# Splitting the expert matrices into high and low parts, slab by slab, in a routed expert layer

## The reference, cut to what matters

```python
s = jax.nn.sigmoid((t @ router_w).astype(jnp.float32))
...
combine = jnp.sum(jax.nn.one_hot(idx, N_EXPERTS, dtype=jnp.float32) * w_sel[..., None], axis=1).astype(dt)
y = jnp.zeros_like(t)
for e in range(N_EXPERTS):
    h = jax.nn.silu(t @ w_gate[e]) * (t @ w_up[e])
    y = y + combine[:, e:e + 1] * (h @ w_down[e])
```

## Time and profile before

| | us |
|---|---|
| median of 3 runs | 3338.19 (3337.83 to 3340.89) |
| the profiled execution | 3339.61 |
| its span | 3337.7 |
| PE busy | 2944.3 (88%) |
| DVE busy | 1571.7 (47%) |
| ACT busy | 962.6 (29%) |
| Pool busy | 383.8 (12%) |
| mean granted TensorE clock | 0.939 of full |

### The profile page before, as it was taken

How to read it: one execution, slowest core, us unless ns; L and a number is a source line. 1 busy time by engine, 2 the same in 40 slices (tenths; PEclk the granted TensorE clock), 3 DMA queues, 4 the chain that set the end, 5 groups by cost and what they waited for, 6 DMA issues and landing times. The chain is left out here.

```text
span 3337.7 us, 56931 instructions
## 1 busy us (share of the span) xinstructions
PE 2944.3 (88%) x25160; PEld 2565.6 (77%) x25160; DVE 1571.7 (47%) x2624; ACT 962.6 (29%) x1623; POOL 383.8 (12%) x238
## 2 busy tenths in 40 slices
PE   6999899898998989998998989989796567699994
PEld 5998898898998979988888989989585554344442
DVE  4633345437886246333454368862378644100003
ACT  4321335323332143213243233321332133001102
POOL 2210121220110002101211101110000100000000
PEclk8999999999998989999999999989897878799997
DMA  6210221462333222102214423332131000888862
GB/s 258 75 43 28 75 76 56 148 220 98 135 133 98 94 80 77 41 28 77 74 56 137 131 89 133 133 110 89 60 95 38 0 19 0 340 341 308 328 224 83
DMA packets 92842, 386.47 MB, mean 116 GB/s; under 512 B 10288, under 2 KB 11312, under 8 KB 85296
## 3 DMA queue, kind: packets, MB, share of 16 engines
q1 hardware_dynamic: 68112, 313.09, 27.0%
q10 hardware_dynamic: 16704, 41.36, 3.4%
q0 software_dynamic: 7776, 28.32, 2.3%
HBM read 332.46 MB, written 50.27 MB: 115 GB/s over the span
## 5 line engine op out<-in xcount | busy, mean ns | idle before, releaser
L307 PE MATMUL PS<-HR,HIGHR 128*128 128x264 f32 x3008 | 864.9, 288 | 0.0
L307 PE MATMUL PS<-XR,HIGHR 128*128 128x264 f32 (+1 forms) x1792 | 570.1, 318 | 48.0 <-DVE HR L1386 14.2
L307 PEld LDWEIGHTS PS<-HR,HIGHR 128*128 128x128 f32 x3008 | 577.9, 192 | 2.9
L307 PE MATMUL PS<-XR,RINGR 128*128 128x264 f32 x1600 | 463.6, 290 | 0.0
L307 PE MATMUL PS<-ARENA 64*64 64x64 f32 (+8 forms) x8640 | 399.6, 236 | 72.1 <-DVE ARENA L2000 43.5
L307 PE MATMUL PS<-HH,HIGHR 128*128 128x264 f32 x1536 | 441.2, 287 | 24.2 <-DVE HR L1603 24.2
L291 ACT CAST HIGHR<-RING 128x1024 fp32r<-128x1024 f32 (+2 forms) x340 | 330.8, 977 | 396.0 <-PE PS L307 293.4
L307 PE MATMUL PS<-HH,RINGR 128*128 128x264 f32 x1536 | 437.9, 285 | 0.0
L307 PEld LDWEIGHTS PS<-ARENA 64*64 64x64 f32 (+5 forms) x8640 | 353.1, 141 | 107.8 <-DVE ARENA L2000 44.9
L307 PE MATMUL PS<-ARENA,RING 128*128 128x512 f32 (+2 forms) x944 | 389.5, 579 | 19.2 <-DVE ARENA L1075 6.5
L307 PEld LDWEIGHTS PS<-XR,HIGHR 128*128 128x128 f32 x1792 | 347.3, 194 | 75.2 <-issue 39.0
(11 more groups left out here) (342 smaller groups left out, 4367.5 us busy)
## 6 DMA issues: line engine op xcount, KB each, us to landing
RING<-wts SPq DMA_DIRECT2D x324, 512.0 KB, 3.6
ARENA<-wmoe SPq DMA_DIRECT2D x51, 2048.0 KB, 9.5
RING<-wts SPq DMA_DIRECT2D x52, 256.0 KB, 2.9
gates<-STAGE ACTq DMA_DIRECT2D x48, 264.0 KB, 4.0
ARENA<-gates ACTq DMA_DIRECT2D x48, 264.0 KB, 2.9
ug<-STAGE POOLq DMA_DIRECT2D x23, 512.0 KB, 14.0
RING<-ug SPq DMA_DIRECT2D x17, 512.0 KB, 10.5
ys<-RING ACTq DMA_DIRECT2D x17, 512.0 KB, 9.5
```

The source lines that it names most:

```text
L307: return e.matmul(out, lhsT, rhs, start=start, stop=stop, skip_group_check=True)
```

## The change

The three matrices of a block become twelve slabs of 128 x 1024 numbers (512 KB): slabs 0 to 3 gate, 4 to 7 up, 8 to 11 down. They go round `NRAW` = 16 raw buffers; eight further buffers (`NSPLIT`) hold high parts. ACT casts each slab to its high part, and the low part is written over the raw slab by Pool for every third slab (2, 5, 8, 11) and by DVE for the other eight. The splitting runs `LEAD` = 6 slabs ahead of PE. The rows and the product are split too, out of PSUM: ACT writes the high part, DVE the low part. Every product is `mm3`. The up product is made in two halves of 256 columns, each in its own PSUM bank, with the product turned in halves as well. The rows get one buffer in place of two, and the product and silu one each.

```diff
+NRAW, NSPLIT = 16, 8
+LEAD = 6
+def of_pool(g):
+    return g % 3 == 2
+def expert_high(k, e, w, g):
...
+    raw, _, high = expert_slab(k, g)
+    w.wait_ge(*k.s[f"expert{g % NRAW}"][g])
+    if g >= NSPLIT:
+        w.wait_ge(*k.s["moe_pe"]["slab", g - NSPLIT])
+    e.copy(high, raw).then_inc(*k.s["moe_act"].done((g // 12, "high", g % 12)))
+def expert_low(k, e, w, g):
...
+    w.wait_ge(*k.s["moe_act"][g // 12, "high", g % 12])
+    e.tensor_tensor(low, raw, high.bitcast(F32), SUB).then_inc(
+        *k.s["moe_pool" if of_pool(g) else "moe_dve"].done((g // 12, "low", g % 12)))
 def block_pe(k, e, w, bk):
...
+    for i in range(4):
+        w.wait_ge(*slab_done(k, 12 * bk + i))
+        ws = slab(i)
+        for q in (2 * i, 2 * i + 1):
+            ins = mm3(e, k.PS[:, b, :], (x[0][:, q, :], x[1][:, q, :]), (ws[0][:, q % 2], ws[1][:, q % 2]), q == 0, q == 7)
+        ins.then_inc(*P.done(("slab", 12 * bk + i)))
...
+        turn_pe(k, e, w, bk + 1)
...
+    for i in range(4):
+        ins = up(0, i)
+    ins.then_inc(*P.done((bk, "first half")))
+    for i in range(4):
+        up(1, i).then_inc(*P.done(("slab", 12 * bk + 4 + i)))
+        if i == 1:
+            turn_product(0)
+    down(0)
+    turn_product(1)
+    for q in range(1, 4):
+        down(q)
 def block_act(k, e, w, bk):
...
+    for i in range(0, 4):
+        expert_high(k, e, w, g + i)
...
+    e.activation(k.SI, k.PS[:, at["gate", bk], :], ACT.Silu).then_inc(*A.done((bk, "silu")))
+    if bk + 1 < NB:
+        turn_act(k, e, w, bk + 1)
+    for i in range(4, 7):
+        expert_high(k, e, w, g + i)
+    turned(0)
+    for i in range(7, 9):
+        expert_high(k, e, w, g + i)
+    turned(1)
+    for i in range(9, 12):
+        expert_high(k, e, w, g + i)
...
     w.wait_ge(*A[bk, "out"])
     w.wait_ge(*V[bk, "out"])
+    e.dma_start(k.ys[128 * bk:128 * bk + 128, :], k.YB[bk % 2]).then_inc(*s[f"result{bk % 2}"].done(bk))
 def block_dve(k, e, w, bk):
...
+    low(0, 1, 3)
+    if bk + 1 < NB:
+        turn_dve(k, e, w, bk + 1)
+    low(4)
+    product(0)
+    turned(0)
+    product(1)
+    low(6)
+    turned(1)
+    low(7, 9, 10)
...
+    e.tensor_copy(k.YB[bk % 2][:, 512:1024], k.PS[:, at["down2", bk] + 1, :]).then_inc(*V.done((bk, "out")))
+def block_pool(k, e, w, bk):
+    for i in (2, 5, 8, 11):
+        expert_low(k, e, w, 12 * bk + LEAD + i)
+def fetch_slabs(k, e, w, bk, which):
...
+        if g >= NRAW:
+            w.wait_ge(*s["moe_pe"]["slab", g - NRAW])
...
+def fetch_sp(k, e, w, bk):
+    fetch_slabs(k, e, w, bk, range(LEAD, 8))
     if bk + 1 < NB:
+        fetch_rows(k, e, w, bk + 1)
+    fetch_slabs(k, e, w, bk, range(8, 12))
+    if bk + 1 < NB:
+        fetch_slabs(k, e, w, bk + 1, range(LEAD))
...
+    for g in range(LEAD):
+        expert_high(k, e, w, g)
+    turn_act(k, e, w, 0)
     blocks(k, e, w, "moe_act", block_act, lambda bk: (f"result{bk % 2}",))
...
+    blocks(k, e, w, "moe_pool", block_pool)
```

More of the change, by code:

```diff
@@ new lines, in turn_act, with turn_dve @@
+def turn_act(k, e, w, bk):
+    for part in range(2):
+        src, (high, low) = rows_of(k, bk, part)
+        if bk >= 2:
+            w.wait_ge(*k.s["moe_pe"]["slab", 12 * (bk - 2) + 7])
+        w.wait_ge(*k.s["moe_pe"][bk, "rows", part])
+        e.copy(high, src).then_inc(*k.s["moe_act"].done((bk, "rows", part)))
+def turn_dve(k, e, w, bk):
+    for part in range(2):
+        src, (high, low) = rows_of(k, bk, part)
+        w.wait_ge(*k.s["moe_act"][bk, "rows", part])
+        e.tensor_tensor(low, src, high.bitcast(F32), SUB).then_inc(*k.s["moe_dve"].done((bk, "rows", part)))
@@ L2343, in block_pe @@
[L2343 to L2350, removed]
+    for part in range(2):
+        w.wait_ge(*V[bk, "rows", part])
+    for i in range(4):
[4 more added lines that the diff above has]
+        ins.then_inc(*P.done(("slab", 12 * bk + i)))
@@ new lines, in turn_product, with down @@
+    def turn_product(half):
+        b = banks.place(w, ("product", bk, half))
+        w.wait_ge(*V[bk, "product", half])
+        for i in range(2):
+            q = 2 * half + i
+            ins = e.transpose(k.PS[:, b, 128 * i:128 * i + 128], k.HB[:, 128 * q:128 * q + 128], k.c("id"))
+        ins.then_inc(*P.done((bk, "turned", half)))
+        banks.emptied_by(b, 1, "moe_dve", (bk, "product low", half))
+    def down(q):
+        if q == 0:
+            banks.place(w, ("down2", bk), 2)
+            banks.emptied_by(banks.at["down2", bk], 1, "moe_act", (bk, "out"))
+            banks.emptied_by(banks.at["down2", bk] + 1, 1, "moe_dve", (bk, "out"))
+        bd = banks.at["down2", bk]
+        w.wait_ge(*V[bk, "product low", q // 2])
+        w.wait_ge(*slab_done(k, 12 * bk + 8 + q))
+        ws = slab(8 + q)
+        for half in range(2):
+            ins = mm3(e, k.PS[:, bd + half, :], (h[0][:, q, :], h[1][:, q, :]), (ws[0][:, half], ws[1][:, half]), q == 0, q == 3)
+        ins.then_inc(*P.done(("slab", 12 * bk + 8 + q)))
@@ L2395, in fetch_sp @@
[L2395 to L2410, removed]
+    g = 12 * bk + LEAD
@@ new lines, in product, with turned @@
+    def product(half):
+        cols = slice(256 * half, 256 * half + 256)
+        if bk:
+            w.wait_ge(*P[bk - 1, "turned", 1])
+        w.wait_ge(*A[bk, "silu"])
+        w.wait_ge(*(P["slab", 12 * bk + 7] if half else P[bk, "first half"]))
+        e.tensor_tensor(k.HB[:, cols], k.PS[:, at["up2", bk, half], 0:256], k.SI[:, cols], MUL).then_inc(
+            *V.done((bk, "product", half)))
+    def turned(half):
+        src, (high, low) = halves_of(k, bk, half)
+        w.wait_ge(*A[bk, "turned", half])
+        e.tensor_tensor(low, src, high.bitcast(F32), SUB).then_inc(*V.done((bk, "product low", half)))
@@ new lines, in low @@
+    def low(*which):
+        for i in which:
+            assert not of_pool(g + i)
+            expert_low(k, e, w, g + i)
+    low(0, 1, 3)
[8 more added lines that the diff above has]
+    low(7, 9, 10)
+    if bk >= 2:
+        w.wait_ge(*s[f"result{bk % 2}"][bk - 2])
+    w.wait_ge(*P["slab", 12 * bk + 11])
+    e.tensor_copy(k.YB[bk % 2][:, 512:1024], k.PS[:, at["down2", bk] + 1, :]).then_inc(*V.done((bk, "out")))
@@ L2447, in blocks_sp @@
             continue
-        names = [f"rows{bk % 2}"] + [f"expert{weight(bk, part)}" for part in range(3)]
+        names = [f"expert{g % NRAW}" for g in range(12 * bk + LEAD, min(12 * bk + LEAD + 12, 12 * NB))]
+        names += ["rows"] if bk + 1 < NB else []
         sent = [(name, s[name].n) for name in names]
@@ L2612, in program_dve @@
     routing_dve(k, e, w)
-    turn_copy(k, e, w, 0, 1, "moe_dve")
+    for g in range(LEAD):
+        if not of_pool(g):
+            expert_low(k, e, w, g)
+    turn_dve(k, e, w, 0)
     blocks(k, e, w, "moe_dve", block_dve)
```

182 lines of the change are left out of this document (89 added, 93 removed).

## The result

The kernel of the change takes 3367.44 us (median of 6 runs, 3358.32 to 3376.06), the kernel before beside it 3339.54 (6 runs, 3337.15 to 3342.88): ratio 1.0085, 95% interval 1.0066 to 1.0104. The profiled execution took 3368.79 us, its span 3367.0. The runs of the new kernel lie 18 us apart, those of the old one 6.

A forecast was written before the change was run, and what follows sets the result against it. PE bounds the kernel before; after the change DVE's list, stopped by Pool's turns, sets 24.5 us a block against 23.12. 16 periods give 22 us, the start 2: 3363.6 us profiled, median 3362, range 3312 to 3392.

The forecast's parts named there:

- The sum: Whole kernel: 16 x (24.5 - 23.12) = 22 us, and 2 for the start, 24 us slower; chance of slower 0.61.
- Start: Start of the expert stage: six slabs cast ahead of the first rows, block 0 some 2 us later (0 to 5).
- End: Behind the last block: Pool's and ACT's passing of six unused blocks each, counted as 0 us, up to 3.
- the port: DVE standing still during Pool's four subtractions a block: 2.25 + 1.85 + 1.7 + 2.25 = 8.05 us.
- PE's share: PE's own work in a new block: products and transposes, 18.2 us, 4.9 less than now.
- The exclusion: DVE and Pool instructions with two SBUF inputs take turns; each Pool subtraction costs DVE up to 2.25 us, 0 to 9.0 a block.
- the walk: DVE's in-order list followed through one block from the end of its result copy, giving a period of 24.5 us.
- the margin that the text named: End of a block: Pool asks for slab 5 at 20.3 us, DVE would take slab 4 at 20.6.
- the first rival: Pool's last grab of a block comes too late to hurt: period 22.25 us, 3326 us in all; chance 0.17.
- PE's stop and the clock: PE stands some 4.5 us a block before the first product half; clock falls to half, period 24.5 against 23.4 without.
- No exclusion: Rival: DVE and Pool don't take turns, a block takes 18.2 + 0.3 us, 3266 us in all; chance 0.07.
- Transfers: Rival: transfers bound the block once Pool does not, 20.5 us by the 358 GB/s limit, 3298 us; chance 0.02.

The follow-up runs named there:

- experiment 2: Kernel of the change with Pool's four low parts a block as plain one-input copies of the raw slab, output not the reference's: 3273.46 us, ratio 0.9796.
- experiment 5: Kernel of the change with one more wait: Pool begins its last subtraction only after DVE has ended its last one: 3338.38 us, ratio 0.9988.
- experiment 3: Kernel of the change with transposes of a constant ahead of PE's wait for the first product half: 3370.2 us with 20, 3367.98 with 28.
- experiment 1: Kernel of the change with all twelve subtractions of a block on DVE and none on Pool: 3307.04 us, ratio 0.990.
- experiment 6: Kernel of the change with PE's conditions nested, so that it jumps once over the unused blocks: 3360.66 us, ratio 1.0053.

## Why the prediction held, and where it didn't

**The sum.** Forecast 24 us on the profiled execution, measured 29. Periods: forecast 24.5, measured 24.31, so 22 against 18.9. Start: forecast 2 (0 to 5), measured 4.8. End: forecast 0 (up to 3), measured 5.3. The median was forecast at 3362 and is 3367.4: the block was right to 1%, and the two ends, 8.1 us over the forecast together, are hidden in part by the 3.1 us that the periods came under it.

That the period came out so near is in part luck. DVE's waits over the 16 periods, which with its busy time make up the whole 388.9 us:

```profile
DVE WR L2319 <- ACT WR L2310: 35.0, 32, 2.1
DVE RING L2478 <- PE PS L308: 23.6, 16, 1.7
DVE HTR L2484 <- ACT HTR L2439: 20.1, 19, 1.3
```

A block: 2.2 us for casts (forecast 1.55 for store and first cast), 1.5 for the second half (2.0), 1.3 for the round by PE and ACT (1.0), 19.4 busy. With 12.3 of its own, 7.1 are left for the port (8.05), and 0.4 had been taken off for start-ups. Terms that were too high and too low nearly cancel.

**PE's share.** 18.2 forecast, 18.13 in four kernels. Right.

**The exclusion.** Right in its price and its place: Pool's turns at 3.5, 7.8 and 14.8 us behind the result copy's end (forecast 3.45, 7.8, 14.65). Over the stage DVE is busy for 310.0 us with it and for 210.6 with the one-input Pool: (310.0 - 210.6) / 16 = 6.2 us a block at least, since that kernel has short turns of its own, and 7.1 by the sum above, where the walk had 8.05. Most of the difference is the fourth turn, which only some blocks pay: DVE is busy for 17.60 us in the block of 22.60 and for 20.02 in the one of 24.10. Its kind was taken too narrowly: it is enough that Pool reads SBUF (experiment 2).

**The walk.** In the block shown (times behind the end of the result copy, 2999.95): slab 7 done at 3.9, slab 9 at 7.25, rows at 8.45, the first half at 11.5, second half 15.4, slab 0 of the next block at 18.3. The forecast was 3.9, 7.1, 8.35, 11.5, 15.4, 18.1. Then it failed by the margin that the text named: slab 5 was cast at 3020.7, 20.8 behind, not 20.3, so DVE went first and the block took 22.6. So the forecast and the first rival are not two outcomes but blocks of one kernel; the order of the turns changes from block to block. The rival's other number, 22.25 for every block, is what experiment 5 measures when the order is forced (22.2).

**PE's stop and the clock.** A stop of some 4.5 us was forecast; there are 5.3, 4.1 and 2.4 in turn. In the three blocks the granted clock is 0.93, 0.85 and 1.00: it falls behind the long stops, as forecast, and not behind the short one. That this costs 1.1 us a block was wrong. The walk had the slow products for slabs 6 and 7 on the path (2.0 us, 0.7 at full clock); the row of the second half above shows DVE waiting 1.73 for them, the mean is 1.5, and with the clock held at 0.99 it is 0.8. So the step was right in kind, but a clock that stays up shortens the wait by 0.7 and not by 1.3, and 0.4 of that is left in the period (experiment 3), within the spread of the runs. Why DVE's own work grows by part of that was not settled; that the turns at the port fall differently would fit, but is argued only.

**The other rivals.** No exclusion: out, by the turns in the rows above and by experiment 1. Transfers: 394 to 401 GB/s over the stage at 18.13 us a block, so they don't bound it there. The Trainium skill (DMA: Bandwidth & Descriptors, Specifications) has some 358 GB/s of HBM for one core, half of what it gives the stack that two cores share; these rows are 10 to 12% above it.

**The start.** The first slab was taken as 3.2 us behind its issue, like the rows before; it was cast at 2868.74, 6.0 behind its issue at 2862.75. That moved PE's first product from 2876 to 2878.4.

**The end.** I had counted the jumps of Pool and of ACT, and not those of PE, whose code per block the change nearly doubles. That is the term that was missing (experiment 6).

## What to carry to other kernels

Before an elementwise operation is shared out to Pool, look at what its neighbour on DVE reads: with two SBUF inputs there, each of the Pool instructions here that met it, with two inputs or one, was a turn taken from DVE, and twelve subtractions on DVE alone were 60 us faster than eight with four on Pool. Walk the list of an in-order engine for the one small instruction that another engine waits for; moving the product ahead of one subtraction gave 37 us, and the best order of all made PE the bound again (3261 us, 2.4% under the kernel before). And count what unused, conditional blocks cost on every engine, above all on the one whose code grew.

## What the runs showed that I had not expected

- Two engines that compete in turns can fall into a pattern of several blocks (24.9, 22.6, 24.1 us); one wait more, on the engine that isn't the bound, made the kernel 29 us faster.
- A one-input copy on Pool, 128x1024, takes 1.15 us beside PSUM work of DVE, against 2.36 for a subtraction, and still takes turns with DVE.
- PE's passing of six unused blocks held the first gather back to 15.4 us behind its last product; jumping once left 6.6.
- A granted clock of 0.92 instead of 0.99 over a stage of 389 us, in which DVE and not PE set the period, makes 6 us between the two executions traced, and nothing that the medians show.
